# Stores and spreads of the S5 responses issued by SyncE in its order of loads, with GpSimd keeping the diagonal products alone

## What is computed

```python
# 128 groups of 16 channels, 64 complex states each, two directions
lam_bar = exp(lam * dt);  b_bar = ((lam_bar - 1) / lam) * B
u, g = split(h @ w_in, 2)
for direction in range(2):
    x[t] = lam_bar * x[t-1] + b_bar @ u[t]        # context first, then latents; flipped for direction 1
    y[t] += real(C @ x[t])
y += d_skip * u
out = ((ya * sigmoid(yb)) * silu(g)) @ w_out      # ya, yb = split(gelu(y) @ w_glu + b_glu, 2)
```

## Time and profile before

| | us |
|---|---|
| median of 3 runs | 1715.08 |
| their lowest and highest | 1708.63, 1732.8 |
| the profiled execution | 1726.91 |
| its span in the trace | 1725.1 |
| mean granted TensorE clock in it | 0.961 |

### The profile page before, as it was taken

The page is one execution under the profiler, slowest core; times in us unless marked ns, Lnnn a source line. Parts: engine busy times, 40 slices in busy tenths (PEclk is TensorE's granted clock), DMA queues, the critical chain, the costliest instruction groups (busy, mean ns, idle before and its releaser), DMA issues.

```text
span 1725.1 us, 26499 instructions
## 1 busy us (share of the span) xinstructions
PE 1574.4 (91%) x10448; PEld 1197.5 (69%) x10448; DVE 725.7 (42%) x1317; ACT 399.7 (23%) x889; POOL 494.6 (29%) x478
## 2 busy tenths in 40 slices
PE   5999899999999679988877999999999999999997
PEld 3444456656544468876766888888788788888786
DVE  6869566665676442276674000011231122333201
ACT  1143433333100120144544000000201011344201
POOL 0169999999860068121110000000000000000000
PEclk8999999999999789998998999999999999999998
DMA  9597877899998347489995444443333332344341
GB/s 389 168 296 235 209 178 175 190 216 217 204 280 268 119 95 221 157 271 317 322 311 172 157 146 147 157 158 122 122 114 107 122 122 98 122 156 160 116 158 43
DMA packets 210761, 316.50 MB, mean 183 GB/s; under 512 B 20080, under 2 KB 179952, under 8 KB 204656
## 3 DMA queue, kind: packets, MB, share of 16 engines
q1 hardware_dynamic: 176736, 221.27, 39.9%
q0 software_dynamic: 26672, 67.55, 16.5%
q10 hardware_dynamic: 7264, 26.43, 4.4%
HBM read 264.98 MB, written 50.20 MB: 183 GB/s over the span
## 4 chain that ended last, share of the span: by engine, by line
PE 51%; DVE 3%; issue 2%; ACT 1%; DVEq 0%; ACTq 0%; PEldq 0%
PE bank L824 25%; PE bank L1137 13%; PE bank L1028 3%; PE bank L1193 2%; PE bank L1064 2%; PE bank L1084 1%; PE bank L1042 1%; PE bank L1160 1%; PE bank L1095 1%; PE bank L1255 0%; PE bank L1076 0%; DVE arena L2196 0%; PE bank L1242 0%; PE bank L1221 0%; PE bank L977 0%
## 5 line engine op out<-in xcount | busy, mean ns | idle before, releaser
L824 PE MATMUL bank<-ht,ring 128*128 128x256 f32 (+1 forms) x1376 | 356.5, 422 | 9.0 <-DVE ht L2198 9.0
L824 PEld LDWEIGHTS bank<-ht,ring 128*128 128x128 f32 x1376 | 263.2, 192 | 100.4 <-issue 70.7
L1137 PE MATMUL bank<-arena,ring 128*128 128x256 f32 x1024 | 222.8, 381 | 1.1 <-PEq L1128 1.1
L1137 PEld LDWEIGHTS bank<-arena,ring 128*128 128x128 f32 x1024 | 195.6, 191 | 28.0 <-issue 1.2
L824 PE MATMUL bank<-gate,ring 128*128 128x256 f32 (+1 forms) x640 | 195.1, 467 | 4.8 <-DVE gate L2250 3.4
L824 PEld LDWEIGHTS bank<-gate,ring 128*128 128x128 f32 x640 | 122.3, 192 | 77.1 <-issue 62.2
L1005 PE MATMUL bank<-ring,ht 128*128 128x256 f32 x512 | 113.8, 384 | 11.9 <-DVE ht L1780 11.9
L1005 PEld LDWEIGHTS bank<-ring,ht 128*128 128x128 f32 x512 | 98.1, 193 | 25.7 <-issue 12.3
L824 PE MATMUL bank<-arena,ring 128*128 128x256 f32 x480 | 106.5, 385 | 3.9 <-DVE arena L2323 3.9
L824 PEld LDWEIGHTS bank<-arena,ring 128*128 128x128 f32 x480 | 92.8, 194 | 17.3 <-DVE arena L2323 4.3
L2170 DVE SCALAR_TENSOR_TENSOR gate<-bank,col,gate 128x256 f32<-128x256 f32 x16 | 7.7, 482 | 195.6 <-ACT gate L1614 195.4
(11 more groups left out here) (361 smaller groups left out, 2312.9 us busy)
## 6 DMA issues: line engine op xcount, KB each, us to landing
ring<-in_s_w_glu SPq DMA_DIRECT2D x32, 1024.0 KB, 5.2
ring<-in_w_mod SPq DMA_DIRECT2D x24, 1024.0 KB, 12.8
ring<-in_w_up SPq DMA_DIRECT2D x22, 1024.0 KB, 5.1
ring<-in_s_w_in SPq DMA_DIRECT2D x16, 1024.0 KB, 9.7
arena<-s_b_powers SPq DMA_DIRECT2D x16, 1024.0 KB, 9.9
arena<-s_b_rows POOLq DMA_DIRECT2D x24, 512.0 KB, 11.5
arena<-s_power_rows POOLq DMA_DIRECT2D x24, 512.0 KB, 12.1
s_b_powers<-arena POOLq DMA_DIRECT2D x24, 512.0 KB, 5.7
```

The costliest lines, as they stand in the source:

```text
L824: mm = pe.matmul(psum[2 * (u % 2) + m][:, 0:mv.free_size()], ring[:, sl, k, m * P:(m + 1) * P], mv, start=(kg == 0 and k == 0), stop=(kg = ...
L1137: mm = pe.matmul(psum[4 * par + 2 * (s // 2) + m][:, 0:S], ring[:, sl, k, m * P:(m + 1) * P], yt[:, kg * 8 + k, :], start=(kg == 0 and k = ...
```

## The change

SyncE issues the stores and spreads, at set places among its loads. GpSimd keeps the diagonal products, in a loop after it has cleared the decay tiles; each waits, as before, for the kfs whose responses read the d_block buffer. The patterns of the DMAs are the same, and so are the semaphores.

```diff
             for s in range(2):
                 load_gate(s)
-            for b in range(3, 5):
-                sp.wait_ge(slot_done, ring_at["s5_u"] + 4 + b)
-                load_cp(b)
+            wide_k = KW5 * BLK
+
+            def store_k(b):
+
+                sp.wait_ge(kf_set, BLK * (b + 1))
+                sp.dma_start(spill_k[b], kf[b % 2][0:2 * CH5].rearrange("p i q c -> p (i q c)")).then_inc(kf_stored[b % 2], 16)
+
+            def spread(b):
+
+                sp.wait_ge(kf_stored[b % 2], 16 * (b // 2 + 1))
+                for g in range(2):
+                    taps = bass.AP(spill_k.tensor, (b * 2 + g) * CH5 * wide_k, [[BLK * CH5, L5], [wide_k, CH5], [1, BLK * P]])
+                    sp.dma_start(t0[b % 2][:, g].rearrange("p i q c -> p (i q c)"), taps).then_inc(t0_in[b % 2], 16)
+
+            store_k(0)
+            sp.wait_ge(slot_done, ring_at["s5_u"] + 7)
+            load_cp(3)
+            sp.wait_ge(ut_done, 14)
+            spread(0)
+            sp.wait_ge(slot_done, ring_at["s5_u"] + 8)
+            load_cp(4)
             for b in range(3):
                 sp.wait_ge(bbd_set, b + 1)
                 load_b(b + 2)
+                if b < 2:
+                    store_k(b + 1)
+                if b == 1:
+                    sp.wait_ge(ut_done, 16)
+                    spread(1)
             sp.wait_ge(in_done, 2)
             load_bm(2)
             load_gate(2)
@@
                 if b + 5 < NB5:
                     sp.wait_ge(y_done, b + 1)
                     load_cp(b + 5)
+                if b + 2 < NB5:
+                    sp.wait_ge(y_done, b + 1)
+                    spread(b + 2)
+                if b + 3 < NB5:
+                    store_k(b + 3)
                 if b % 2 and b < 14:
                     load_gate((b + 5) // 2)
@@
-            def store_k(b):
-            ...
-            def spread(b):
-            ...
-            store_k(0)
-            spread(0)
-            store_k(1)
             pool.wait_ge(slot_done, ring_at["s5_g"])
             pool.wait_ge(gl_set, 1)
             pool.memset(dec5[0], 0.0).then_inc(p_link, 1)
             pool.memset(dec5[1], 0.0).then_inc(p_link, 1)
             pool.wait_ge(p_link, count[0] + 4)
             pool.sem_inc(decays_clear, 1)
-            spread(1)
-            store_k(2)
-            for b in range(NB5 - 2):
-                spread(b + 2)
-                if b + 3 < NB5:
-                    store_k(b + 3)
+            for b in range(2, NB5):
+                pool.wait_ge(kf_set, BLK * (b - 1))
+                diagonal(b)
```

More of the change, by code:

```diff
@@ L2454, in _ @@
             pool.tensor_scalar(xl[:, :, :], xl[:, :, :], ALPHA, None, ALU.mult).then_inc(alpha_set, 1)
-            wide_k = KW5 * BLK
-            def store_k(b):
[L2459 to L2462, removed]
-            def spread(b):
[L2466 to L2473, removed]
-            store_k(0)
-            spread(0)
-            store_k(1)
             pool.wait_ge(slot_done, ring_at["s5_g"])
```

## The result

| | before | after |
|---|---|---|
| median, us | 1732.38 | 1743.85 |
| lowest to highest | 1708.63 to 1742.06 | 1728.26 to 1747.96 |
| runs | 20 | 20 |
| the profiled execution's span | 1725.1 | 1742.2 |

The ratio is 1.0088, 95% interval 1.0063 to 1.0113: the change costs some 15 us, under the 2% that I had set as the bound of "slower", but well outside no change. The same kernel measured again gave 1.0067 (1.0034 to 1.01). The kernel before itself had a median of 1732 over 20 runs, where the three that I had seen gave 1715.

What follows compares the result with a forecast made beforehand. Full DMA engines were taken to set PE's pace, through late instructions or loads. Start +2, DMA -1 and -1 in all were summed to 0 on the execution's 1725.1, 12 over the median: forecast 1715, range 1692 to 1738.

Steps and rivals of the forecast that it cites:

- the start: Before S5's loop: load_b(2) lands later behind the first spread, responses(2) starts 1.2 to 2.8 us late; taken as +2 us.
- -1 in all: S5's loop: DMA work on eight engines, 143 us against 144, with some short stalls perhaps gone; taken as -1 us.
- GpSimd's relief, its clears, diagonal(2): GpSimd in S5: 48 fewer DMA issues, clears up to 3 us earlier, diagonal(2) some 13 us later; all cost 0.
- SP's issues: SP in S5's loop: the 48 moved issues add 1.7 us to a block of 12 us, hidden.
- Waits in the loop: SP's new waits in S5's loop, for kfs and for a store's landing, delay no load; cost 0.
- my point of 13.7: S5's loop: a store's landing would have to take over 13.7 us to hold up the next bm load.
- that of 21.7: S5's loop: store landing of about 21.7 us, from which late trig loads decide the time.
- The DMA engines: S5's loop, twelve blocks: all bytes in SP's queue, spreads on eight engines, 143 us of DMA work against 144; -1 us.
- The rule that I set beside the row: Skill's rule: a copy uses the largest engine number up to 16 dividing both outermost counts; SP's spreads load the same eight.
- the two bounds: DMA work of twelve S5 blocks: 120 us with spreads over 16 engines, 143 us over the same eight.
- The fourth: Rival: in S5's loop SP waits for late store landings, bm and trig go out late; 1743 us, chance 0.08.
- The third: Rival: in S5's loop the eight engines carrying the spreads need 162 us, +18, with the start 1735 us; chance 0.18.

## Why the prediction was wrong

I forecast 1715 us and no change. Measured are 1743.85, above the range's end of 1738, and the ratio excludes 1.0. Two steps failed: the start, which was put at +2 and cost 7.4, and the base. The sum itself has a slip: the two terms that the text gives, +2 and "-1 in all", make +1, and the -1 is counted twice in it. Step by step:

*GpSimd's relief, its clears, diagonal(2): 0.* Right. After, PE's and ACT's waits name none of them.

*SP's issues: hidden.* Right for 3 issues of a block; SP's timeline has idle time in each block. The run with 16 small DMAs a block shows where that ends.

*The start: +2.* The step that failed for the change. The issue time was nearly right (2.4 us late against my 2). The landing was mis-sized: I let 0.5 MB of spread pass at the clean rate of 396 GB/s, 1.3 us, and it took 3.9 us more, with 213 GB/s moved while load_b(2) was in flight. responses(2) started 4.2 us late where I had 1.2 to 2.8. And I put no price on what an idle PE costs afterwards: 2.2 us at the lower clock, and 1.0 behind it. The sum is 7.4.

*Waits in the loop: 0.* Nearly right in its effect, wrong in its reason. I compared with stores that land in 8.0 us at the median and 12.3 at most in GpSimd's queue. In SP's queue, behind the loads (L684, 700 to 945):

```profile
DMA to landing us min/median/max: 1.9/9.8/14.7
```

That is above my point of 13.7 in two blocks, below that of 21.7 in all. But SP waited 67.6 us for these landings, in 14 waits, and the spreads, which I had going out within 1 us after each outputs(b), did so once and then went 1.8 to 14.4 us after it. Putting the store first gained 2 us of loop.

*The DMA engines: -1.* The loop moved by +0.5, so the size was right, by luck: two large changes cancelled. The stalls at PE fell by 13.8 us, which I had let stand as possible and mostly not taken; the late loads took the same back. That PE's stalls go with full DMA engines is not settled either: they were 13.6 us with two queues and the 16-engine spread, 16.5 with one queue and eight DMAs a spread. The rule that I set beside the row, eight engines, was the right choice between the two bounds (9 completions for each of SP's spreads; with an outermost count of 128 they are 16). But I drew the wrong thing from it. The clean rate of 25.5 KB per engine-us of the earlier trace rows is that of transfers over 128 partitions, not of "one queue". Mixing queues does not set it for the most part: with the same two queues the 16-engine spread over 128 partitions is worth 19.5 us (176.8 to 157.3), with SP's queue alone 25.7 (177.3 to 151.6). Of the 25.7 the number of engines has 5 to 14, as above; of the 19.5 it has nothing (177.4).

*The rivals.* The fourth, "SP's queue blocks", has the nearest time, 1743, by luck: its chain was there (7% of the execution's path are store landings), but at a price of about 2 us and not 26, and on a base 17 us too low. The third, eight engines as the bound, at 1735, came closest in its signs: DVE waits 40.0 us for trig, over the 30 that I had named as its sign, with the engines at 0.93 to 0.95. But its place was wrong, as the loop's length hardly changed, and its cause has only a part: with 16 engines and the same bytes GpSimd's queue gained nothing. "Supply wins" gave what it named (fewer stalls) and no time.

*The base.* I took 1715 as the kernel before; its median over 20 runs is 1732. That is the larger part of the 29 us between forecast and result; the same range laid about 1732 would end at 1755 and hold the result. My own sum stood on an execution of 1726.91 and I took 12 us off it to meet three runs.

**What stays open.** The start explains 7 us of the 12 to 15 that the ratios show. The loops of the two profiles differ by 0.5 us, but one profile is one execution. Mending the start leaves 1.0032 (0.9997 to 1.0068), and with the store first as well 1.0057 (1.0024 to 1.0091), which excludes 1.0 though its profile has start and loop 2 us shorter than before. So some 5 to 10 us of loss are left by the ratios and aren't located.

## What to carry to other kernels

When DMA engines are full, ask of each transfer over how many partitions and engines it goes, before asking in which queue it stands: one that is split unlike the rest slowed all of them here, and a load over 128 partitions cut by partitions came later, not earlier. Before a small load that the first matmuls of a stage need, put nothing that can wait, however hidden it looks in the loop; here part of the idle time was paid again in clock. Take the time before from the execution that the argument stands on, or widen the range by what its few runs leave open.

## What the runs showed of the hardware that I had not expected

- Cutting a 1 MB load of 128 partitions into two DMAs of 64 slowed the whole traffic of the loop from 314 to 254 GB/s and the kernel by 2.45% (1.8 to 3.1).
- The same bytes in the same queue took 87 or 128 ns for each 2 KB packet, as one DMA over 128 partitions or as two over 64. Steps between rows of 256 or 512 bytes, and rows stored 3840 or 4096 bytes apart, made no gain.
- PE's stalls without a releaser (4.76 us at once), which I read as late instructions, went from 25.6 us to 11.8 when one queue moved the bulk, and were back at 24.1 with the spreads on GpSimd's. But they were 13.6 there with the 16-engine spread, so the number of queues alone does not set them.
- After 4.16 us of idle PE the granted clock was 0.53 for the next 5.6 us.
